# A transformer layer with 32 routed experts: the last expert's rows are added by products instead of a scatter, and one attention copy changes its engine

## The reference

```python
o = diff_attention(...)             # 4 heads, two maps each, all keys
o = swa_context / swa_latent(...)   # 8 heads over a window
x = x + g1 * rms_norm(merge_branches(oa, ob, ga, gb, p), g_post_mix)

def hierarchical_moe(h, p):
    g_sel = argmax(lg)                              # one of 4 groups
    top_v, top_i = top_k(le_sel, 2)                 # two of its 8 experts
    w_pair = g_w * softmax(top_v)
    y = routed_experts(t, e_id, w_pair, w1, w3, w2)

def blk(xb, w_b, e):                                # per expert and its tokens
    hb = silu(xb @ w1[e]) * (xb @ w3[e])
    return (hb @ w2[e]) * w_b[:, None]              # added to the token's row

x = x + g2 * rms_norm(hierarchical_moe(h, p), g_post_ffn)
```

## Time and profile before

| | before |
|---|---|
| three runs | 1274.02, 1275.89, 1275.96 us |
| median | 1275.89 us |
| the profiled execution's own time | 1276.03 us |
| its span in the trace | 1274.3 us |
| TensorE busy | 1143.4 us, 90% |
| VectorE busy | 844.3 us, 66% |
| ScalarE busy | 695.0 us, 55% |
| GpSimd busy | 316.4 us, 25% |
| granted TensorE clock, mean | 0.953 of full speed |

### The profile page before, as it was taken

One profiled execution on the slowest core, in us unless ns is written; L12 is line 12 of the kernel. 1 busy time (PEld: TensorE's weight loads), 2 busy tenths in 40 slices (PEclk: granted clock), 3 DMA queues, 4 the chain that ended last, 5 costly groups with the idle time before them and its releaser, 6 DMA issues. The chain is left out here.

```text
span 1274.3 us, 16835 instructions
## 1 busy us (share of the span) xinstructions
PE 1143.4 (90%) x5943; PEld 919.6 (72%) x5943; DVE 844.3 (66%) x901; ACT 695.0 (55%) x787; POOL 316.4 (25%) x306
## 2 busy tenths in 40 slices
PE   3889999999787998999669999999999999999960
PEld 2567788777566786888558888888888888888850
DVE  3543133113687663643858998989998999889945
ACT  3223223223565452124448777877788777878733
POOL 4032021000212001000223344334433443334200
PEclk9889999999799799999879999999999999999985
DMA  9624334555000214441389999999999999999916
GB/s 311 240 100 149 135 122 153 173 177 178 27 1 10 77 65 165 125 141 34 116 286 388 379 370 375 380 359 358 353 368 362 352 351 371 363 358 356 373 58 248
DMA packets 146029, 296.39 MB, mean 233 GB/s; under 512 B 12097, under 2 KB 13250, under 8 KB 145330
## 3 DMA queue, kind: packets, MB, share of 16 engines
q1 hardware_dynamic: 130656, 265.83, 58.3%
q0 software_dynamic: 15152, 29.73, 7.0%
q10 hardware_dynamic: 162, 0.05, 0.0%
HBM read 290.68 MB, written 27.95 MB: 250 GB/s over the span
## 5 line engine op out<-in xcount | busy, mean ns | idle before, releaser
L1218 PE MATMUL psum<-w_hi,act_hi 128*128 128x512 f32 (+1 forms) x1288 | 516.3, 401 | 22.9 <-DVE w_lo L1918 6.4
L1220 PE MATMUL psum<-w_hi,act_lo 128*128 128x512 f32 (+1 forms) x1288 | 501.8, 390 | 0.0
L1219 PE MATMUL psum<-w_lo,act_hi 128*128 128x512 f32 (+1 forms) x1288 | 501.2, 389 | 0.0
L1218 PEld LDWEIGHTS psum<-w_hi,act_hi 128*128 128x128 f32 x1288 | 244.2, 190 | 95.8 <-issue 18.1
L1220 PEld LDWEIGHTS psum<-w_hi,act_lo 128*128 128x128 f32 x1288 | 244.2, 190 | 51.8
L1219 PEld LDWEIGHTS psum<-w_lo,act_hi 128*128 128x128 f32 x1288 | 244.8, 190 | 45.1
L1918 DVE TENSOR_TENSOR w_lo<-raw_extra,w_hi 128x2048 fp32r<-128x2048 f32 x96 | 217.2, 2290 | 45.6 <-ACT w_hi L1094 45.6
L1918 DVE TENSOR_TENSOR w_lo<-raw_mix,w_hi 128x2048 fp32r<-128x2048 f32 x96 | 219.0, 2288 | 12.3 <-ACT w_hi L1094 12.3
L1094 ACT ACTIVATE w_hi<-raw_mix 128x2048 fp32r<-128x2048 f32 x96 | 184.0, 1917 | 35.5 <-PE psum L1220 26.8
L1094 ACT ACTIVATE w_hi<-raw_extra 128x2048 fp32r<-128x2048 f32 x96 | 180.7, 1913 | 6.6 <-PE psum L1220 6.6
L1630 DVE TENSOR_TENSOR w_lo<-raw_mix,w_hi 128x2048 fp32r<-128x2048 f32 (+1 forms) x24 | 52.8, 2202 | 166.3 <-ACT w_hi L894 166.3
(11 more groups left out here) (276 smaller groups left out, 1172.4 us busy)
## 6 DMA issues: line engine op xcount, KB each, us to landing
raw_mix<-in_w_e SPq DMA_DIRECT2D x96, 1024.0 KB, 8.1
raw_extra<-in_w_e SPq DMA_DIRECT2D x96, 1024.0 KB, 7.9
raw_mix<-in_w_in SPq DMA_DIRECT2D x16, 1024.0 KB, 6.0
raw_mix<-in_w_ada SPq DMA_DIRECT2D x16, 1024.0 KB, 6.8
ada_first<-in_w_ada SPq DMA_DIRECT2D x8, 1024.0 KB, 20.4
gates_scratch<-rows POOLq DMA_DIRECT2D x20, 256.0 KB, 2.7
yrow<-gates_scratch POOLq DMA_DIRECT2D x20, 256.0 KB, 4.5
raw_mix<-in_w_out SPq DMA_DIRECT2D x4, 1024.0 KB, 5.2
```

The costliest lines, as they stand in the source:

```text
L1218: pe.matmul(out, a_hi(ka_), w_hi[:, kw, :], start=s, stop=False)
L1219: pe.matmul(out, a_hi(ka_), w_lo[:, kw, :], start=False, stop=False)
L1220: ins = pe.matmul(out, a_lo(ka_), w_hi[:, kw, :], start=False, stop=e)
```

## The change

**The last expert.** Expert 31's rows aren't scattered in the first round. `all_scattered` is raised as soon as the scatters of experts 0 to 30 have landed, and the pair rows are reloaded from there; the count's load and the branches come behind the stores, in one outer branch. The rows of `y_scratch` that expert 31 would have written have to be zero, so the table is filled with zeros early (a transfer from a zeroed tile `lam`, between two weight loads of the branch projections). A 128x640 matrix `last_onehot` holds, for each slot of the last expert, its weight in its token's column. For each tile TensorE adds into two PSUM banks the matrix times `ysb` and the identity times VectorE's pair sum, in fp32; square and gate read the sum from there.

**The roots.** ScalarE takes a square root per tile behind its square, VectorE inverts it, and a final row is made as soon as its tile is ready, with gating, next sum, reciprocal and final row in turn. Output rows are stored from the raw slots and no longer from `xrow`.

**Attention.** The fifth key tile of the differential steps is copied by ScalarE.

The diff's core:

```diff
         def copier(i, j):
-            return "act" if (steps[i][0] == "diff") == (j == 0) else "dve"
+            return "act" if steps[i][0] == "diff" or j else "dve"
...
             for n in range(1, NU):
+                if n == NU - 5:
+                    sp.wait_ge(const_made, 2)
+                    sp.dma_start(y_d.rearrange("(p a) (b c) -> p (a b) c", p=P, c=256), lam[:, :].unsqueeze(1).broadcast_to([P, 40, 256])).then_inc(final_out, 16)
                 load_unit(n)
...
+            def pairs(again):
+                for i in range(NT):
+                    if not again:
+                        sp.wait_ge(lo_done, NS + UPR - 5 + i)
+                    sp.dma_start(raw_pair(i), y_d[2 * P * i:2 * P * (i + 1), :].rearrange("(p k) n -> p (k n)", k=2)).then_inc(x_in[i], 16)
+                for i in range(NT):
+                    sp.wait_ge(c_out, NT * again + i + 1)
+                    sp.dma_start(y_dst[i], raw_pair(i)[:, 0:D]).then_inc(final_out, 16)
...
             a_round(0)
+            sp.wait_ge(all_scattered, 1)
+            pairs(0)
             sp.wait_ge(cnt_done, 1)
...
                 scatter(b + NE - 2, 0, (b + NE - 2) // 2)
-                scatter(b + NE - 1, 1, (b + NE - 2) // 2)
-                for j in range(2):
-                    po.wait_ge(moe_sc[j], 16 * (b + NE) // 2)
+                if r:
+                    scatter(b + NE - 1, 1, (b + NE - 2) // 2)
+                po.wait_ge(moe_sc[0], 16 * (b + NE) // 2)
+                po.wait_ge(moe_sc[1], 16 * (b + NE) // 2 - (0 if r else 16))
 
             a_round(0)
+            po.sem_inc(all_scattered, 1)
...
+            def pair_root(i, again):
...
+                ac.activation(pt[:, 1024:2048], rows_, ACT.Square, scale=1.0 / 32, accum_out=stat[:, i:i + 1]).then_inc(c_sq, 1)
+                ac.wait_ge(c_sq, n + 1)
+                ac.activation(stat[:, 8 + i:9 + i], stat[:, i:i + 1], ACT.Sqrt, bias=eps[:, 0:1]).then_inc(c_rs, 1)
...
+            for i in range(NT):
+                if i >= 3:
+                    pe.wait_ge(c_gate, i - 2)
+                    pe.wait_ge(c_sq, i - 2)
+                for x in range(2):
+                    pe.matmul(bank(SUM_BANK[i] + x), loh[:, i * P:(i + 1) * P], ysb[:, D + x * 512:D + x * 512 + 512], start=True, stop=False)
+                pe.wait_ge(c_sum, i + 1)
+                for x in range(2):
+                    ins = pe.matmul(bank(SUM_BANK[i] + x), ident[:, :], raw_pair(i)[:, x * 512:x * 512 + 512], start=False, stop=True)
...
-                if diff:
-                    columns(i)
...
+            parts = last_parts[:, :].rearrange("p (x n) -> p x n", n=3)
+            link(ve.tensor_tensor(last_w[:, :], ohw[:, :].rearrange("p (x n) -> p x n", n=NE)[:, :, NE - 1], wk[:, :], ALU.mult))
...
+            def last_expert_onehot():
...
+                for i in range(NT):
+                    ins = ve.tensor_scalar(loh[:, i * P:(i + 1) * P], cidx[:, :], last_tok[:, 1 + i:2 + i], last_slot_w[:, 0:1], ALU.is_equal, ALU.mult)
...
+                if r == 0:
+                    last_expert_onehot()
                 expert(r, NE - 1, 1, NE // 2 - 1 + NE * r // 2, True)
```

More of the change, by code:

```diff
@@ L640, in a_round @@
                 body(r, NE - 1, s0 - 3 + 6 * (NE - 1), None)
+            def pairs(again):
[6 more added lines that the diff above has]
+                    sp.dma_start(y_dst[i], raw_pair(i)[:, 0:D]).then_inc(final_out, 16)
+                sp.wait_ge(final_out, 16 + 16 * NT * (1 + again))
             a_round(0)
+            sp.wait_ge(all_scattered, 1)
+            pairs(0)
             sp.wait_ge(cnt_done, 1)
             most = sp.value_load(cnt_i[0:1, 0:1], min_val=0, max_val=TOK)
[L645 to L656 removed]
+            with sp.If(most > P):
+                a_round(1)
+                for r in range(2, ROUNDS):
+                    with sp.If(most > P * r):
+                        a_round(r)
+                sp.wait_ge(all_scattered, 2)
+                pairs(1)
             sp.wait_ge(kv_out, 16 * 4)
@@ L1045, in _ @@
                         ac.activation(pt[:, a:a + w], bank(6)[:, 0:w], ACT.Copy).then_inc(pt_act, 1)
+                copied([j for j in range(len(groups(i))) if copier(i, j) == "act"])
                 for q in flush.get(i, []):
@@ L1546, in _ @@
             slot_table(0)
+            pe.wait_ge(last_weights, 2)
+            parts = last_parts[:, :].rearrange("p (x n) -> p x n", n=3)
+            for x in range(2 * NT):
+                ins = pe.matmul(bank(7)[:, P:P + 3], roc[:, x * P:(x + 1) * P], parts[:, x, :], start=(x == 0), stop=(x == 2 * NT - 1))
+            ins.then_inc(last_weight_mm, 1)
             def transpose_x(n, par, pair):
@@ L1608, in _ @@
             a_round(0)
+            pe.wait_ge(last_onehot, 3)
+            pe.wait_ge(moe_ya, NE)
+            pe.wait_ge(moe_yv, NE)
+            for i in range(NT):
+                if i >= 3:
[6 more added lines that the diff above has]
+                    ins = pe.matmul(bank(SUM_BANK[i] + x), ident[:, :], raw_pair(i)[:, x * 512:x * 512 + 512], start=False, stop=True)
+                ins.then_inc(c_mm, 1)
             pe.wait_ge(cnt_done, 1)
             most = pe.value_load(cnt_i[0:1, 0:1], min_val=0, max_val=TOK)
-            for r in range(1, ROUNDS):
-                with pe.If(most > P * r):
-                    slot_table(r)
-                    a_round(r)
+            with pe.If(most > P):
+                pe.wait_ge(c_gate, NT)
+                pe.wait_ge(c_sq, NT)
+                slot_table(1)
+                a_round(1)
+                for r in range(2, ROUNDS):
+                    with pe.If(most > P * r):
+                        slot_table(r)
+                        a_round(r)
         @block.vector
@@ L2082, in _ @@
+            a_round(0)
+            ve.wait_ge(g2_in, 32)
+            pair_sum(0, 0)
+            pair_sum(1, 0)
+            for i in range(NT):
+                pair_gate(i, 0)
+                if i + 2 < NT:
+                    pair_sum(i + 2, 0)
+                final_rows(i, 0)
             ve.wait_ge(cnt_done, 1)
             most = ve.value_load(cnt_i[0:1, 0:1], min_val=0, max_val=TOK)
-            for r in range(1, ROUNDS):
-                with ve.If(most > P * r):
-                    ve.tensor_scalar(round_pos[:, :], slot_pos[:, :], -float(P * r), None, ALU.add).then_inc(round_done, 1)
-                    ve.wait_ge(round_done, r)
-                    slot_table(r, round_pos)
-                    a_round(r)
@@ L2105, in _, with again @@
-            ve.wait_ge(g2_in, 32)
-            for i in range(NT):
-                pair_sum(i)
-            for i in range(NT):
-                final_rows(i)
+            with ve.If(most > P):
+                for r in range(1, ROUNDS):
+                    def again(r=r):
+                        ve.tensor_scalar(round_pos[:, :], slot_pos[:, :], -float(P * r), None, ALU.add).then_inc(round_done, 1)
+                        ve.wait_ge(round_done, r)
+                        slot_table(r, round_pos)
+                        a_round(r)
+                    if r == 1:
+                        again()
+                    else:
+                        with ve.If(most > P * r):
+                            again()
+                for i in range(NT):
+                    pair_sum(i, 1)
+                    pair_gate(i, 1)
+                    final_rows(i, 1)
```

145 lines of the change are left out of this document (91 added, 54 removed).

## The result

| | before | changed |
|---|---|---|
| first session, median | 1274.95 us (4 runs, 1271.85 to 1275.96) | 1255.62 us (4 runs, 1255.52 to 1256.07) |
| ratio to before, 95% interval | | 0.9852 (0.9835 to 0.9869) |
| a later session, median | 1274.09 us (7 runs) | 1258.37 us (4 runs, 1252.62 to 1260.72) |
| ratio there | | 0.9881 (0.9865 to 0.9898) |
| profiled execution: span | 1274.3 us | 1254.3 us |

The first four runs agree within 0.6 us; in the later session four runs spread over 8.

The account below looks back on a forecast made before the run. A serial tail (last scatter, landing, reload, VectorE's sums) bounds the kernel. VectorE from 1241.2 plus 17.5 gives 1258.7; plus 3.47 and 1.0, 1263.2; minus 1.5 attention, plus 1.73 around the span: 1263.5 us, range 1258.5 to 1269.5.

Parts of the forecast that it names:

- the attention term: Differential attention steps: moving the fifth tile's copy to ScalarE saves 0.4 us a tile, 1.5 us over four tiles.
- the bound of −4.5: Attention's most favourable case: all the copy time VectorE sheds, 16 times 0.28 us, comes off the total.
- Reload issued 8.1 ahead: Kernel end: pair-row loads go out from 1225.95, 16 us earlier, with 3.57 us for the preceding scatter to be seen.
- First square ended 7.1 behind: Kernel end, ScalarE: tile 0's square out of PSUM takes 1.2 us and ends at 1241.2.
- VectorE's run 17.5: Kernel end: five gatings, three sums, five reciprocals and five final rows without gaps from 1241.2 to 1258.7.
- Behind it 4.5: After VectorE's last final rows: 3.47 us as before, plus 1.0 for the count's load and one branch (bounds 0.9 and 1.8).
- Costed at nothing: The y_scratch fill, POOL's zeroing, the last expert's weights and its one-hot hide behind other work and add no time.
- 1, the table switch: Rival at the end: ScalarE's table switch drains the pipeline, costing 1.3 us more; 1264.8 us, chance 0.15.
- 2: Rival in attention: the fifth copy blocks ScalarE in short steps, +3.6 us instead of −1.5; 1268.6 us, chance 0.09.
- 3: Rival at the end: loads land later or in another order, VectorE's chain starts 2 to 3 us later; 1266, chance 0.07.
- 4: Rival at the end: TensorE's twenty products run at 1.2 GHz; 1277.8 us, or some 1271 if half; chance 0.05.
- 5: Rival before the projections: the 1 KB-piece fill delays a weight load; at 116 us it costs 55; 1318, chance 0.03.

Follow-up runs that it names:

- experiment 1: Kernel before with the attention copy alone moved to ScalarE, its end unchanged: 1270.03 us median against 1274.65, ratio 0.9971.
- experiment 5: Kernel before with ScalarE copying the fifth tile also in the last tile's four differential steps only: 1274.12 us against 1275.04, ratio 0.9993.
- experiments 2 to 4: 2: changed kernel, attention copy back on VectorE, 1260.98 us; 3: kernel before, sixteen small VectorE operations before attention, 1277.22 us; 4: changed kernel again, 1258.37 us.
- experiment 6: Changed kernel with SP's load of the count behind the five reloads instead of behind the stores: 1257.6 us median.
- experiment 8: Changed kernel with the reload held until both halves of the last expert's rows are copied: 1267.71 us, ratio 0.9955.

## Why the prediction was wrong

**The step that failed is the attention term, and in it the multiplication.** It read one tile's four steps, found −0.4 and took four times that. From one tile's output to the next (us):

| tile | before | changed | copy alone (1) | last tile alone (5) |
|---|---|---|---|---|
| second | 18.43 | 17.28 | 19.21 | 19.36 |
| third | 15.97 | 15.43 | 15.41 | 15.73 |
| fourth | 15.98 | 15.60 | 15.60 | 15.96 |
| last | 15.42 | 13.19 | 13.18 | 13.90 |
| together | 65.80 | 61.50 | 63.40 | 64.95 |

The read tile was about right: 15.97 became 15.43, −0.5, and the next −0.4. But the first of the four won 1.15 and the last 2.2. In the last, TensorE waited 1.7 us at a stretch for VectorE's copy, and some 2 us later its clock fell for 3.4 us; without the wait it didn't (experiment 5). So the differential steps gave −4.3, near the bound of −4.5 that the text had for another reason. This is no accident of one execution: six of the seven traces with the copy in all steps have 61.5, the seventh 63.4 (experiment 1), and the three without it 65.7 to 66.5. A granted clock of 0.89 stands in the view of the last tile, 391.31 to 406.73; the forecast looked at the clock only where the kernel ends. What made the 1.15 of the first of the four wasn't tried.

**No term for low clock in untouched code.** The forecast was made against one execution with 24 us of low clock between 396 and 500, 17 of them in one piece that cost 5.9 to 6.5 us. The changed kernel's profiled execution had 17 us there, and the two stretches with the same code took together 73.6 instead of 76.5 us. These −2.9 are luck of two executions, shown by experiments 2 to 4, and it belongs into the width of the range, not into its middle: runs of one kernel lay 8 us apart (1271.33 to 1279.18; 1252.62 to 1260.72), and the range had no allowance for that; the three runs that it was made from lay 2 us apart.

**What each adds.** The forecast had 12.6 us less of span, the profiled executions have 20.0. The 7.4 between them are 2.8 of the differential steps, 2.9 of low clock in untouched code, 1.5 of the end and 0.2 elsewhere. None alone puts the time below 1258.5.

**The end, step by step**, counted from VectorE's last copy (forecast, measured in the changed kernel):

- Reload issued 8.1 ahead, was 9.9 ahead: the 3.57 us of the earlier trace rows between scatter and its being seen became at most 1.8 (scatter issued until 1214.99, first load at 1216.78). Why the last scatter before took longer wasn't tried.
- Tile 3's rows 4.8 behind, were 2.7 behind.
- Products 0.86, were 0.86; tile 0 summed 4.2 behind, was 4.5. TensorE was never held, so all ended 18.3 behind, not 19.3.
- First square ended 7.1 behind, was 5.7, since the landings no longer held it; 1.2 for a square out of PSUM was 1.1.
- VectorE's run 17.5, was 16.3: 1.22, 1.27, 0.15 and 1.28 for gating, sum, reciprocal and final row make 17.1, since a reciprocal took 0.15 and not 0.25. The rest is overlap of neighbours of up to 0.08, 0.7 together, of the 1.0 that the text allowed and left out of the sum.
- Behind it 4.5, was 5.5: the count's load and branch are 1.3 (experiment 6), in the bounds of 0.9 and 1.8, not 1.0; and the last store landed in 3.71 us, not in the 3.02 of the kernel before.

Together 29.1 forecast, 27.6 measured. The errors partly cancel. Two sums of the text are a little off, which changes nothing: 1261.7 and 1.73 make 1263.4, not 1263.5, and a fill of 116 us against the text's cover of 63.6 or 59 would cost 52 or 57, not 55.

**Costed at nothing.** The fill went out at 326.14, long before the 444 of its place in the queue: SP waited only for GpSimd's zeroed tile (325.79 + 0.33). It took 16.8 us, and nobody waited for it. The one-hot ended at 1215.05 and the product behind it still found VectorE idle for 0.82 us, waiting for TensorE. Both as forecast, the fill with more room.

**The rivals.** 1, the table switch: the load took 1.28 and the next activation started 0.02 us behind it (1232.38, 1233.68 above), no drain in this trace either, and the second square, at 1234.92, was in time. 2 fell: attention won. 3 fell: the loads were earlier. 4 fell: the clock was full while TensorE had products in the end; it fell only at 1250, behind them. 5 fell: the fill took 16.8 us, not over 59.

## What to carry to other kernels

Before scaling a reading from one iteration to all, look at the granted clock and at the longest single wait of TensorE in each iteration: here the one with a wait of 1.7 us and a low stretch behind it carried half of the gain. Judge an edit at the end of a program by the stretch from a fixed event to the end, not by the total, where the total moves by 8 us through the clock; and put that spread into the range. Where results of many producers are gathered through memory, starting the reload before the last producer and adding its share by a small product made the end 12.6 us shorter here, 9.5 of which were lost again when the reload was held back.

## What the runs showed of the hardware

- In the differential steps, between the first tile's output and the last's, single waits of TensorE of 1.7 to 1.9 us were followed by 3.4 or 6.8 us at 1.2 GHz within 0.6 to 2.6 us, six of six over the traces; the last tile's wait of 1.7, three of three. A wait of 1.6 us just ahead of the first tile's output was followed by 3.4 us low in eight traces and by none in two (experiments 1 and 3). None of the waits of 1.2 to 1.5 us in these steps was.
- In the windowed steps behind them the low time of identical code was 0, 3.4, 6.8, 10.2 or 17.1 us from trace to trace.
- Low clock costs less than half of itself there: against the trace without it 3.4 us low are 0.6 to 0.8 us of time, 17.1 are 6.5.
- A reload of 5 MB in five pieces landed 15.1 us after its first issue beside a working TensorE (changed kernel) and 14.6 with TensorE idle (experiment 8): 4.7 us for the first piece, then one every 2.5 us but for 2.9 between the first two in the changed kernel. The kernel before took 17.4 us, with 5.1 between the first two; why isn't known.
- The mean granted clock of a run goes with its time: of 21 runs of the kernel before, the one at 0.948 took 1279.18, five at 0.949 to 0.953 took 1275.81 to 1276.03, those at 0.959 and 0.960 took 1271.33 and 1272.01.
- Reading a count into a register and branching on it behind the last store's landing took 1.3 us.
